# Two short DVE steps of an expert placed one weight split earlier in a mixture-of-experts kernel

## What is computed

```python
out = jnp.zeros((T, D), jnp.float32)
for e in range(N_EXPERTS):                      # 16, T = 576, D = 1024, hidden 512
    y = (jax.nn.silu(t @ w_g[e]) * (t @ w_u[e])) @ w_d[e]
    out = out + gate[:, e:e + 1] * y.astype(jnp.float32)
```

## Time and profile before

| what | value |
|---|---|
| median of 3 runs | 708.25 us (707.78 to 708.43) |
| the profiled execution | 708.4 us |
| its span, first to last instruction | 706.5 us |
| PE busy | 682.2 us (97%) |
| DVE busy | 522.6 us (74% of the span) |
| ACT busy | 425.0 us (60%) |
| POOL busy | 143.0 us (20%) |
| mean granted TensorE clock | 0.993 |

### The profile page before, as it was taken

One profiled execution on the slowest core, in us unless ns is written; L12 is line 12 of the kernel. 1 busy time (PEld: TensorE's weight loads), 2 busy tenths in 40 slices (PEclk: granted clock), 3 DMA queues, 4 the chain that ended last, 5 costly groups with the idle time before them and its releaser, 6 DMA issues.

```text
span 706.5 us, 9504 instructions
## 1 busy us (share of the span) xinstructions
PE 682.2 (97%) x3514; PEld 546.1 (77%) x3514; DVE 522.6 (74%) x686; ACT 425.0 (60%) x607; POOL 143.0 (20%) x161
## 2 busy tenths in 40 slices
PE   8999999999999999999999999999999999999992
PEld 4899788777676777788878778888888888888871
DVE  5347654565887674665557998899999999988884
ACT  6746734244664443553333478888888888888881
POOL 4202850021001110100001202222222222222235
PEclk9999999999999999999999999999999999999997
DMA  8724232403771000230185699999999999999844
GB/s 302 244 95 160 92 141 83 168 0 135 282 301 72 1 1 2 88 120 1 39 350 167 234 419 403 398 389 376 380 380 376 383 386 387 378 386 387 306 152 165
DMA packets 33155, 161.23 MB, mean 228 GB/s; under 512 B 6221, under 2 KB 6555, under 8 KB 18396
## 3 DMA queue, kind: packets, MB, share of 16 engines
q1 hardware_dynamic: 23680, 140.40, 51.0%
q0 software_dynamic: 5344, 10.27, 5.6%
q10 hardware_dynamic: 4092, 10.07, 3.9%
HBM read 149.59 MB, written 20.03 MB: 240 GB/s over the span
## 4 chain that ended last, share of the span: by engine, by line
PE 78%; DVE 14%; ACT 3%; issue 2%; DMA 1%; POOL 1%; POOLq 0%; SPq 0%; ACTq 0%; DVEq 0%
PE pj L2206 39%; PE scores L2206 20%; PE tr_v L2206 12%; DVE wl L1479 4%; PE tr_a L2214 2%; PE scores L2675 2%; DVE w_lo L1508 2%; PE tr_a L2704 1%; PE tr_v L2214 1%; DVE hid L1479 1%; DMA raw<-in_dense 1%; ACT w_hi L979 1%; DVE w_lo L1479 1%; POOL rs L779 1%; DVE tiny L1742 0%
## 5 line engine op out<-in xcount | busy, mean ns | idle before, releaser
L1479 DVE TENSOR_TENSOR wl<-moe_raw,wh 128x2048 fp32r<-128x2048 f32 x96 | 218.6, 2291 | 23.8 <-ACT wh L937 23.0
L937 ACT ACTIVATE wh<-moe_raw 128x2048 fp32r<-128x2048 f32 x96 | 182.2, 1919 | 32.8 <-PE scores L2206 12.0
L777 POOL TENSOR_SCALAR rs<-stat 128x1 f32<-128x1 f32 (+4 forms) x31 | 13.7, 443 | 307.9 <-DVE stat L1700 151.9
L2206 PE MATMUL pj<-w_hi,xT_hi 128*128 128x512 f32 (+2 forms) x176 | 64.1, 364 | 0.9 <-ACT w_hi L979 0.8
L831 POOL DMA_INDIRECT acc_rows<-y,idx_sb x14 | 22.2, 1589 | 205.5 <-ACT y L1401 205.5
L2206 PE MATMUL pj<-w_hi,xT_lo 128*128 128x512 f32 (+2 forms) x176 | 61.9, 352 | 0.0
L2206 PE MATMUL pj<-w_lo,xT_hi 128*128 128x512 f32 (+2 forms) x176 | 60.8, 352 | 0.0
L2206 PE MATMUL pj<-wh,xgh 128*128 128x512 f32 x128 | 51.5, 402 | 0.5 <-issue 0.5
L2206 PE MATMUL tr_v<-wh,xgh 128*128 128x512 f32 x128 | 51.1, 399 | 0.0
L1508 DVE SCALAR_TENSOR_TENSOR w_lo<-raw,pack_a,w_hi 128x512 fp32r<-128x512 f32 (+2 forms) x64 | 43.9, 745 | 9.4 <-ACT w_hi L979 9.3
L2206 PE MATMUL scores<-wh,hTh 128*128 128x512 f32 x128 | 49.9, 390 | 0.6 <-DVE hTl L1479 0.6
(11 more groups left out here) (458 smaller groups left out, 1522.3 us busy)
## 6 DMA issues: line engine op xcount, KB each, us to landing
moe_raw<-in_w_exp_gate SPq DMA_DIRECT2D x32, 1024.0 KB, 7.1
moe_raw<-in_w_exp_up SPq DMA_DIRECT2D x32, 1024.0 KB, 7.7
moe_raw<-in_w_exp_down SPq DMA_DIRECT2D x32, 1024.0 KB, 7.4
raw<-in_dense SPq DMA_DIRECT2D x16, 1024.0 KB, 6.4
raw<-in_dense SPq DMA_DIRECT2D x8, 256.0 KB, 6.3
x_rows<-in_x_prompt SPq DMA_DIRECT2D x4, 512.0 KB, 10.8
xw<-in_x_prompt ACTq DMA_DIRECT2D x1, 2048.0 KB, 8.2
h_rows<-h ACTq DMA_DIRECT2D x4, 512.0 KB, 3.7
```

The source lines that it names most:

```text
L777: link(pool.tensor_scalar(rs[rows, n, cs], stat[rows, n, cs], EPS, None, ALU.add))
L937: act.activation(wh[s4][:, :], moe_raw[n % RING][:, :], ACT.Copy).then_inc(hi_done, 1)
L1479: return dve.tensor_tensor(out, a, b, op)
L2206: return pe.matmul(out, lhsT, rhs, start=start, stop=stop, skip_group_check=True)
```

## The change

In the loop of DVE's `step`, `hidden` stands before `split_lo` 4 instead of before `split_lo` 5; `hid_lo` stands before `split_lo` 5 instead of before `split_lo` 6; and the part of the overflow list, so far behind the loop, stands between them, just ahead of `hid_lo`. No instruction is added or removed, and no wait is changed. The branch for the last expert and the loop for extra rounds are as they were.

```diff
                 for j in range(3, 9):
+                    if j == 4:
+                        hidden(e, 6 * e + 4)
                     if j == 5:
-                        hidden(e, 6 * e + 4)
-                    if j == 6:
+                        if 2 <= e <= 10:
+                            extra_lists(e - 2)
                         hid_lo(e, b)
                     if e == E - 2 and j == 6:
                         dve.wait_ge(last_tok_T, 1)
                         dve.tensor_scalar(shared[:, :], px[0][:, 0:P], next_tok, None, ALU.is_equal).then_inc(shared_ready, 1)
                     split_lo(e, b, j)
-                if 2 <= e <= 10:
-                    extra_lists(e - 2)
```

## The result

The changed kernel takes 704.59 us (median of 6 runs, 703.9 to 705.39), the kernel before 708.31 us beside it (6 runs, 707.78 to 709.13). The ratio is 0.9945, 95% interval 0.9933 to 0.9957: 3.7 us faster. The profiled execution took 704.19 us with a span of 702.3.

A forecast was written before the change was run, and what follows sets the result against it. The prediction took PE to bound the kernel, waiting once per step for `hid`. Gains of 2.86, 0.33 and 0.07 us sum to 3.26: 708.4 to 705.1, forecast 705.0 us as median, range 704.3 to 706.3.

The forecast's parts named there:

- What bounds the kernel: Expert stage: PE sets the pace at 17.98 us a step, with one wait per step, for `hid`, costing 0.22 us.
- The place of `hidden`: DVE ahead of split 4: `hidden` waits some 0.15 us for up, then ends 1.8 us before PE wants it.
- The size: Whole gain from PE's ended waits for `hid` in steps 0 to 14: 3.26 us, 3.5 at the upper end.
- the gap of steps 1 to 13: PE's idle time ahead of the transposes at `hid_turn`: 0.22 us in each of 13 steps, 2.86 us.
- `hid_lo` ahead of split 5: On DVE, `hid_lo` ends about 545.85 instead of 546.78; spare time ahead of down grows from 0.5 to 1.2 us.
- The overflow list: Ahead of `hid_lo` on DVE, its longest part of 0.98 us fills an existing wait; at most 0.05 us delay.
- Splits 5 to 8 and VectorE's round: Split 5 keeps 1.7 us ahead of down's second unit; later splits hide in DVE's slack, 16.0 to 16.7 of 17.76 us.
- The rival of the transfers: Weight loads from HBM already set the pace, so the step stays at 17.98 us: 708.3 us, chance 0.06.
- The half-gain rival: Another wait, for the gather or the up bank, takes half the gain: 706.6 us, chance 0.07.
- The slower rival: Split 5, behind `hid_lo`, comes late for down's second unit; one whole split late gives 713.9 us, chance 0.03.
- the prediction's 12 us of lead: Load into split 4's freed slot lands within 7.7 us, at 551.1; ACT reads it at 563.2, 12 us to spare.

The follow-up runs named there:

- even_steps: Kernel before with `hidden` and `hid_lo` moved ahead in even steps alone, list at the end of the step: 706.15 us, ratio 0.9967 to the kernel before.
- hid_late: Against the kernel before, `hidden` and `hid_lo` put behind split 5, list at the end of the step: 745.81 us, ratio 1.0538.
- hid_only: Against the kernel before, only `hidden` moved ahead of split 4; `hid_lo` and the list at their old places: 709.6 us, ratio 1.001.
- low_longer: Changed kernel with `hid_lo`'s subtraction repeated ahead of it on 512 and 384 columns: 710.02 us, ratio 1.0033 to the kernel before.
- low_between: Changed kernel with `hid_lo`'s subtraction repeated ahead of it on 512 and 128 columns: 706.75 us, ratio 0.9978 to the kernel before.
- list_back: Changed kernel with the overflow list left at the end of the step: 704.74 us, ratio 0.9954 to the kernel before.
- more_full: Changed kernel with all of split 5 done twice, behind `hid_lo`: 717.75 us, ratio 1.0139 to the kernel before.
- more_half: Changed kernel with half of split 5 done twice, behind `hid_lo`: 704.63 us, ratio 0.9956 to the kernel before.
- low_and_list_only: Against the kernel before, `hidden` stays; the list and `hid_lo` go right behind it, ahead of split 5: 708.32 us, ratio 0.9996.

## Why the prediction was right, and where it was off

**What bounds the kernel** was right: one gap per step, at `hid_turn`, in a stage that TensorE sets. even_steps and hid_late show that it is VectorE's order that makes it, step by step.

**The place of `hidden`** was right: it starts 0.05 to 0.1 us behind up's end and waits 0.17 (0.15 was said). The transposes no longer wait in any of the 15 steps.

**The size was too small**: 3.26 us against 3.85 in the loop and 3.7 measured. The term that was mis-sized is the gap of steps 1 to 13, taken as 0.22 us each. It measured 0.26 by the steps. The prediction compared the distance ahead of the transposes alone (0.46 against 0.24; it became 0.23) and left out the transposes themselves, which take 0.36 us when their weight loads are ahead of them and took 0.41 when they weren't. The row for it stood in its own groups: a weight load waiting for `hid`, not a matmul. The two together are 0.28, of which 0.02 doesn't show in the step. Times 13 that is 0.5 of the 0.6 us missed; steps 0 and 14 give the rest (0.39 and 0.13 instead of 0.33 and 0.07).

**"`hid_lo` ahead of split 5"** was kept as a safe move, but its part was not seen, and two numbers of it are off. The spare time before was put at 0.5 us; by the prediction's own times it is 547.07 - 546.78 = 0.29. And it did not work out the time without the move: with `hidden` ahead, `hid_lo` comes 0.52 us closer to its due time (0.24 behind the last gate matmul's start in hid_only, 0.28 ahead of it before), and that is more than it had. hid_only measured it: all the gain lost. The other number is the spare time after. The prediction held the new `hid_lo` and split 5 against down's old due times, 547.07 and 549.79, but with the gap gone down comes 0.28 us sooner. So 1.2 us is 0.95 (543.43 to 544.38; 1.02 in steps without a list). Of that, 1.3 us more is too much (low_longer), and 1.05 more is at the edge (low_between).

**The overflow list** costs nothing at either place (list_back), as said.

**Splits 5 to 8 and VectorE's round** were right in kind; the room of 1.7 us is 1.5 (more_full), again the 0.28 us by which down comes sooner, and 1.1 of it can be used for nothing (more_half).

**The rival of the transfers** fell: ScalarE never waited for a load, and the mean rate rose with the shorter step, from 385 to 389 GB/s. The rule of the Trainium skill, "DMA: Bandwidth & Descriptors", "Where 436 GB/s comes from", that 358 GB/s per core binds is not borne out here, with the kernel on one core.

**The half-gain rival** did not come either: nothing else waits. **The slower rival** needs 2.2 us more work on VectorE to appear.

The Trainium skill's page "TensorE: Matmul & The Clock Gate", section "Step-by-step: what each phase is for", says that TensorE pulls a weight load ahead of matmuls in flight. The trace agrees, with the load for the transposes at 541.17, 0.23 us ahead of them. In the kernel before, `hid` wasn't there in time, the loads started together with the transposes at 544.03, and the four transposes took 0.05 us more: the part of the term that the prediction left out.

## What to carry to other kernels

When a small step is moved ahead on an engine, work out the due time of every step that it is moved past, and of the next small step behind those, with the due times of the shorter step: here the earlier `hidden` took 0.52 us from `hid_lo`, which had 0.28, and half of the change alone gained nothing. Date an operand's due time to the weight load, one matmul ahead (here a load up to 0.12 us late was free), and count what the sequencer still computes between the wait and the load. Measure a gap from the last matmul before it to the first full one behind, so that slower transposes or loads in between are counted. A step that waits for another engine is the place for work that is wanted by nobody soon: up to 1 us of list fitted there for nothing.

## What the runs showed beyond that

- The granted clock fell to its lower level behind 3 of the 15 waits in hid_late (distances 2.94, 2.67 and 2.67 us), while the other twelve (2.5 to 2.78) left it at full speed; the loss was 1.5 us each. Why these three, no run here tells.
- Down's first matmul waits for `hl_done`, though `hTl` is first read by the third, whose load comes 0.35 us after the first's in hid_only (`scores<-wh,hTl` at 548.84). A wait ahead of the third matmul, or one that stands behind those for `y_done` and `lo_done`, would give `hid_lo` more time. No run here tried it.
- The loads land later in the changed kernel, though it moves the same bytes. Landing times of the weight loads from 440 to 655, before and then after:

```profile
DMA to landing us min/median/max: 6.4/7.3/9.6
```

```profile
DMA to landing us min/median/max: 6.1/7.9/11.8
```

The gathers too take 10.7 us in the median instead of 9.6. It goes with the four splits behind `hid_lo`, which now free their slots back to back, 2.2 us apart, and not with the shorter step: low_and_list_only, whose step is as long as before, has 7.8 and 10.8 us in the median. It cost nothing; the prediction's 12 us of lead had reckoned with loads that land within 7.7 us.
